# Two-stack hybrid network on one core: the second stack's opening norm in feature-major blocks, and a new order of the first microseconds

## The reference

```python
def hybrid_layer(x, ...):              # first stack
    h = rms_norm(x, norm_gain)
    proj = h @ w_in                    # attention in two kinds, gates ...
    y = sigmoid(gate_a) * (ua @ w_branch_a) + sigmoid(gate_b) * (ub @ w_branch_b)
    return x + y @ w_out

def second_block(x, meta_tokens, ln_in_g, ln_in_b, ...):
    h = concatenate([meta, x], axis=1)          # 16 + 256 tokens
    h = _layer_norm(h, ln_in_g, ln_in_b)        # mean and variance over the 2048 features
    for l in range(DEPTH):
        h = _hybrid_layer(h, pos, ...)          # convolution, windowed attention, recurrence
    return h[:, N_META:]                        # ends each layer in a _layer_norm too
```

## Time and profile before

| | us |
|---|---|
| median of the runs shown (3) | 3278.61 |
| lowest, highest | 3278.15, 3279.22 |
| the profiled execution, its own time | 3277.46 |
| its span, first to last instruction | 3275.7 |
| PE busy in that span | 3215.3 |
| DVE, ACT, POOL busy | 1989.7, 1652.3, 497.6 |

### The profile page before, as it was taken

How to read it: one execution, slowest core, us unless ns; L and a number is a source line. 1 busy time by engine, 2 the same in 40 slices (tenths; PEclk the granted TensorE clock), 3 DMA queues, 4 the chain that set the end, 5 groups by cost and what they waited for, 6 DMA issues and landing times.

```text
span 3275.7 us, 48063 instructions
## 1 busy us (share of the span) xinstructions
PE 3215.3 (98%) x17364; PEld 2782.6 (85%) x17364; DVE 1989.7 (61%) x2226; ACT 1652.3 (50%) x2291; POOL 497.6 (15%) x426
## 2 busy tenths in 40 slices
PE   8999999999999999999999999999987999999998
PEld 7888888888888888888888888888877999989997
DVE  5666655455544555766755555544546887668966
ACT  5445456555344445444555555444434566455654
POOL 4544500000000003554500000000002000010000
PEclk9999999999999999999999999999998999999998
DMA  6555555545655555555555555555553444544443
GB/s 230 173 173 183 174 169 173 179 160 179 193 193 192 186 200 181 173 173 173 184 174 171 170 175 173 193 193 193 186 169 139 153 139 139 174 170 150 153 155 116
DMA packets 157148, 566.90 MB, mean 173 GB/s; under 512 B 17536, under 2 KB 19728, under 8 KB 156752
## 3 DMA queue, kind: packets, MB, share of 16 engines
q1 hardware_dynamic: 155680, 558.00, 51.2%
q0 software_dynamic: 1344, 7.16, 0.6%
HBM read 562.99 MB, written 2.10 MB: 173 GB/s over the span
## 4 chain that ended last, share of the span: by engine, by line
PE 96%; DVE 2%; ACT 1%; POOL 1%; issue 0%; DMA 0%; SPq 0%; ACTq 0%; POOLq 0%; DVEq 0%
PE acc L1602 23%; PE acc L1604 23%; PE acc L1603 23%; PE acc L1856 6%; PE acc L1858 6%; PE acc L1857 6%; PE work L1662 1%; PE work L1835 1%; PE work L1919 1%; DVE w_lo L1023 1%; PE work L1836 1%; PE work L1837 1%; PE work L1947 0%; PE work L1719 0%; PE work L1670 0%; PE work L1673 0%
## 5 line engine op out<-in xcount | busy, mean ns | idle before, releaser
L1023 DVE TENSOR_TENSOR w_lo<-raw,w_hi 128x1024 fp32r<-128x1024 f32 x1056 | 1399.6, 1336 | 1025.7 <-ACT w_hi L606 870.9
L606 ACT ACTIVATE w_hi<-raw 128x1024 fp32r<-128x1024 f32 x832 | 874.4, 1057 | 903.3 <-PE acc L1604 903.3
L1602 PE MATMUL acc<-w_hi,hT_hi 128*128 128x512 f32 x2560 | 1014.7, 396 | 2.4 <-DVE hT_lo L1029 2.4
L1604 PE MATMUL acc<-w_hi,hT_lo 128*128 128x512 f32 x2560 | 999.0, 390 | 0.0
L1603 PE MATMUL acc<-w_lo,hT_hi 128*128 128x512 f32 x2560 | 997.5, 390 | 0.0
L1604 PEld LDWEIGHTS acc<-w_hi,hT_lo 128*128 128x128 f32 x2560 | 481.0, 188 | 102.9
L1602 PEld LDWEIGHTS acc<-w_hi,hT_hi 128*128 128x128 f32 x2560 | 481.6, 188 | 97.5 <-issue 2.8
L1603 PEld LDWEIGHTS acc<-w_lo,hT_hi 128*128 128x128 f32 x2560 | 481.8, 188 | 95.8
L620 ACT ACTIVATE w_hi<-raw 128x1024 fp32r<-128x1024 f32 x224 | 236.2, 1057 | 298.8 <-PE acc L1858 286.1
L1856 PE MATMUL acc<-h_hi,w_hi 128*128 128x272 f32 (+1 forms) x1152 | 336.5, 292 | 0.0
L1858 PE MATMUL acc<-h_hi,w_lo 128*128 128x272 f32 (+1 forms) x1152 | 329.9, 286 | 0.0
(11 more groups left out here) (314 smaller groups left out, 3636.8 us busy)
## 6 DMA issues: line engine op xcount, KB each, us to landing
raw<-weights SPq DMA_DIRECT2D x1056, 512.0 KB, 3.3
mat<-mats POOLq DMA_DIRECT2D x2, 1536.0 KB, 7.5
X<-x_in SPq DMA_DIRECT2D x8, 256.0 KB, 7.3
out<-out_rows SPq DMA_DIRECT2D x8, 256.0 KB, 2.5
par<-params POOLq DMA_DIRECT2D x2, 640.0 KB, 5.0
cst<-consts POOLq DMA_DIRECT2D x1, 704.0 KB, 4.8
cst<-consts POOLq DMA_DIRECT2D x1, 552.0 KB, 4.7
ropeC<-rope POOLq DMA_DIRECT2D x2, 256.0 KB, 5.1
```

Source lines behind the costliest of these rows:

```text
L606: act.activation(w_hi[:, slot, :], raw[:, slot, :], ACT.Copy).then_inc(hi_ready, 1)
L1023: dve.tensor_tensor(w_lo[:, s % RING, :], raw[:, s % RING, :], w_hi[:, s % RING, :], ALU.subtract)\
L1602: pe.matmul(o, stat[0][:, kc, token], hi, start=(kc == 0), stop=False)
L1604: ins = pe.matmul(o, stat[1][:, kc, token], hi, start=False, stop=(kc == KC - 1))
```

## The change

**Between the stacks.** The token-major norm is taken out. During the last output projection, as soon as a block of 512 features has been added to `X`, PE transposes it (`turn_in`, two feature blocks at a time) between the halves of the next blocks. ACT evacuates the first two turns, DVE the others. The mean over the first 512 features, times a factor (`shift`), is subtracted from everything, so that sums of squares stay small. Sums of the centred blocks and of their squares are gathered on DVE (`sum_in`, `in_sum`), the squares on ACT (`square_in`), and PE adds them up over the partitions with `ones_d` (`mean_part`). After the last block two more turns, two evacuations, two squares and one sum follow, and then the same routine as between the layers (`variance`, `normal_pairs` on DVE, `norm_root_of`, `high_pairs` on ACT), now written once for both. `h2` moves in memory to where `ubT` was, so that `F` and `PJ` come next to each other. POOL issues its three DMAs and sets its constants when the last `yT_lo` is made, which is ahead of most of the projection. The chunks of `first_half` no longer have transposes between them.

**At the start.** `kept` is loaded ahead of the first weights. DVE clears `U`; ACT makes an activation on one column of it, which brings its table load to the front; PE makes six products on it (`FIRST_WARM`). The first slot of weights is split in two halves of 512 columns, and PE's first six products wait only for the first of them (`first_lo`).

```diff
@@ SP
             sp.dma_start(cst[:, C_ID:C_ID + P], consts1[:, C_ID:C_ID + P]).then_inc(set_loaded, 16)
+            sp.dma_start(kept[:, :, :], kept1).then_inc(set_loaded, 16)
             for slot in range(RING):
                 sp.dma_start(raw[:, slot, :], weights[slot]).then_inc(raw_loaded[slot], 16)
-                if slot == 0:
-                    sp.dma_start(kept[:, :, :], kept1).then_inc(set_loaded, 16)
@@ POOL
-            pool.wait_ge(x_added, 4 * DEPTH)
+            pool.wait_ge(y_ready, 4 * DEPTH)
+            pool.wait_ge(yT_lo, 8 * DEPTH)
             pool.dma_start(cst2[:, :], consts2).then_inc(in2_loaded, 16)
@@ ACT, start
+                    act.wait_ge(const_set, 2)
+                    act.activation(small[:, 90:91], U[:, 0, 0:1], ACT.Copy)
                     act.wait_ge(set_loaded, 32)
-                    for f in range(8):
+                    act.wait_ge(raw_loaded[0], 16)
+                    act.activation(w_hi[:, 0, 0:512], raw[:, 0, 0:512], ACT.Copy).then_inc(first_hi, 1)
+                    h_hi(l, 0)
+                    act.activation(w_hi[:, 0, 512:HALF], raw[:, 0, 512:HALF], ACT.Copy).then_inc(hi_ready, 1)
+                    for f in range(1, 8):
                         split(u, f, f + 1)
                         h_hi(l, f)
@@ ACT, last projection and opening norm
+            def evac_in(f):
+                act.wait_ge(turned2, f + 1)
+                act.activation(F[:, 2 * f:2 * f + 2, META:TOK], work[:, f, :].rearrange("p (c n) -> p c n", c=2), ACT.Copy)\
+                    .then_inc(in_raw, 1)
+            def square_in(p, centered):
+                act.wait_ge(in_centered, centered)
+                act.activation(sqf[:, 2 * p:2 * p + 2, :], F[:, 2 * p:2 * p + 2, :], ACT.Square).then_inc(in_sq, 1)
...
+            act.activation(small2[:, 1:2], small2[:, 2:3], ACT.Sqrt)
+            square_in(6, 8)
+            square_in(7, 9)
+            act.wait_ge(in2_loaded, 48)
+            norm_root_of(0)
+            split2(3)
+            high_pairs(0, 0)
@@ DVE, end of the last projection
+            split(g0 + 18, 15, 16)
+            sum_in(6, sqf[:, 0:2, :], sqf[:, 0:2, :], sqf[:, 4:6, :])
+            dve.wait_ge(in_centered, 7)
...
+            sum_in(12, LNT[:, 3, :], sqf[:, 0, :], sqf[:, 1, :])
+            for n in range(3):
+                split(U2, n, n + 1)
+            dve.wait_ge(acc_ready, U2)
+            for a in range(2):
+                x = X[:, :, 1536 + 256 * a:1792 + 256 * a]
+                dve.tensor_tensor(x, acc[:, 2:4, 256 * a:256 * a + 256], x, ALU.add).then_inc(x_added, 1)
+            evac_in(6)
+            evac_in(7)
+            dve.wait_ge(in_sq, 8)
+            sum_in(13, sqf[:, 12:14, :], sqf[:, 12:14, :], sqf[:, 14:16, :])
...
+            normal_pairs(0, 0)
@@ PE, start
+                    pe.wait_ge(const_set, 2)
+                    for _ in range(FIRST_WARM):
+                        pe.matmul(work[:, 3, 0:256], U[:, 0, 0:P], U[:, 1, :], start=True, stop=True)
@@ PE, last projection
+            def turn_in(f, added):
+                pe.wait_ge(x_added, added)
+                for c in (2 * f, 2 * f + 1):
+                    for t in range(NT):
+                        o = c % 2 * SEQ + t * P
+                        ins = pe.transpose(work[:, f % 4, o:o + P], X[:, t, c * P:c * P + P], ident)
+                ins.then_inc(turned2, 1)
+            def mean_part(bank, src, start, stop):
+                return pe.matmul(work[:, bank, 0:TOK], ones_d[:, :], src, start=start, stop=stop)
...
+            out_halves(3, 0, 2)
+            turn_in(4, done + 3)
+            out_halves(3, 2, 3)
+            turn_in(5, done + 3)
+            out_halves(3, 3, 7)
+            pe.wait_ge(in_sum, 12)
+            mean_part(0, LNT[:, 0, :], True, False)
+            mean_part(1, LNT[:, 3, :], True, False)
+            out_halves(3, 7, 8)
+            turn_in(6, done + 4)
+            turn_in(7, done + 5)
...
-                    if l == 0 and kc + 4 < KC:
-                        turn_x(kc + 4)
```

More of the change, by code:

```diff
@@ L107 @@
 PREP = 32
+FIRST_WARM = 6
 def releases():
@@ L797, in _ @@
                 split(g0 + 16, 6, 13)
[L798 to L801, removed]
+                if l + 1 < DEPTH:
+                    for n in range(3):
+                        for f in (2 * n, 2 * n + 1):
+                            split(g0 + 16 + n, 13 + f % 2, 14 + f % 2)
                             h_hi(l + 1, f)
-                    split(g0 + 16 + n, 15, 21 if n < 2 else 16)
@@ L806, in square_in @@
[L806 to L813, removed]
-                split2(n)
[L815 to L819, removed]
+                        split(g0 + 16 + n, 15, 21 if n < 2 else 16)
@@ new lines, in _, with norm_root_of, scale_pair @@
+            square_in(0, 4)
+            split(g0 + 17, 18, 19)
+            square_in(1, 5)
+            split(g0 + 17, 19, 21)
+            split(g0 + 18, 13, 16)
+            square_in(4, 6)
+            square_in(5, 7)
+            def norm_root_of(q):
+                act.wait_ge(post_var, 2 * (q + 1))
+                k = FROM[q - 1] if q else 0
+                act.activation(rs2[:, k:TOK], rs2[:, k:TOK], ACT.Sqrt).then_inc(norm_root, 1)
+            def scale_pair(q, p):
+                act.wait_ge(post_mul, 8 * q + p + 1)
+                k = FROM[q - 1] if q else 0
+                for c in (2 * p, 2 * p + 1):
+                    f = F[:, c, k:TOK]
+                    gain, offset = (par2[:, a + c:a + c + 1] for a in (R2_POSTG, R2_POSTB)) if q else (gin[:, a + c:a + c + 1] for a in (0, KC))
+                    act.activation(f, f, ACT.Identity, scale=gain, bias=offset).then_inc(f_ready, 1)
@@ L1223, in _ @@
                             h_lo(l + 1, f)
-                    split(g0 + 16 + n, 15, 20 if n < 2 else 16)
-                if l + 1 < DEPTH:
+                        split(g0 + 16 + n, 15, 20 if n < 2 else 16)
                     split(g0 + 20, 0, 3)
-                add_x(l, 3)
-            dve.wait_ge(x_added, 4 * DEPTH)
-            dve.wait_ge(set2, 5)
-            groups = [(X[:, n, :], P) for n in range(NT)] + [(meta_rows[:, :], META)]
-            for n, (src, r) in enumerate(groups):
-                if n == 2:
-                    dve.wait_ge(in2_loaded, 48)
-                dve.tensor_reduce(mean_in[0:r, n:n + 1], src, AX.X, ALU.add).then_inc(in_sum, 1)
@@ L1237, in _ @@
[L1237 to L1245 removed]
+                    add_x(l, 3)
@@ L1263, in keys, with normal_pairs @@
+            def normal_pairs(q, n):
+                variance(q, 0)
+                for p in range(1, KC // 2):
+                    if p > 1:
+                        subtract(q, p, 0)
+                    multiply(q, p, 0)
+                    low(q, p - 1)
+                    if 2 <= p < 7:
+                        split2(n + 1 + p)
+                low(q, KC // 2 - 1)
+            normal_pairs(0, 0)
             def keys(l):
@@ new lines, in mean_part @@
+            def mean_part(bank, src, start, stop):
+                return pe.matmul(work[:, bank, 0:TOK], ones_d[:, :], src, start=start, stop=stop)
+            done = 4 * (DEPTH - 1)
+            pe.wait_ge(yb_ready, 4 * DEPTH)
+            out_halves(1, 0, 2)
+            turn_in(0, done + 1)
+            out_halves(1, 2, 3)
+            turn_in(1, done + 1)
+            pe.wait_ge(in2_loaded, 48)
+            for c in range(KC):
+                ins = pe.transpose(work[:, 2, c * META:c * META + META], meta_rows[:, c * P:c * P + P], ident[0:META, 0:META])
```

325 lines of the change are left out of this document (199 added, 126 removed).

## The result

| | before | after |
|---|---|---|
| median, us | 3278.38 (4 runs, 3277.11 to 3279.22) | 3257.35 (4 runs, 3256.16 to 3259.89) |
| ratio, 95% interval | | 0.9937 [0.9926, 0.9949] |
| profiled execution: time, span | 3277.46, 3275.7 | 3257.23, 3255.4 |

What follows compares the result with a forecast made beforehand. PE was taken to bound the kernel (96% of the last chain). −17.2 − 6.6 + 1.0 + 7.2 − 1.7 − 2.7 = −20.0 us gave 3257.4 for the profiled execution, median 3258.6 us, range 3253.5 to 3265.

Steps and rivals of the forecast that it cites:

- start, first product and clock: Kernel start: first product at 9.4 instead of 11.1, −1.7 us; warming products lift the clock, −2.7 us.
- what the projection takes on: Last projection: PE takes on six turns (3.2), sixteen `meta_rows` transposes (2.6) and three `ones_d` products (1.4), together +7.2 us.
- hole: Between the stacks: last product seen by DVE to next stack's first product shrinks from 29.6 to 12.4 us, −17.2 us.
- chunks with the clock: First 16 chunks of the second stack: 12 groups of transposes shed, −6.6 us; extra low clock, +1.0 us.
- the squares' path: Between the stacks: ACT, DVE, PE, DVE handling of squares arrives last ahead of `rs2`, formed at 5.3 us.
- Half of the low-clock time: Behind the hole: extra low clock of 0 to 2.8 us, half of it lost; +1.0 us taken.
- the term of the sixteen transposes of `meta_rows`: In the projection: 0.16 us each, from a range of 0.135 to 0.28; 2.6 us in all, at most 4.5.
- The tight place: Ahead of the last projection half: DVE's sums stand at 9.8 us, PE asks at 10.9, 1.1 us to spare.
- Rival 2: Projection waits because sums or splits are late by more than 1.1 us: 3260 to 3264 us, chance 0.12.
- two forecast terms: Kernel start: earlier first product, −1.7 us, and clock already lifted at that product, −2.7 us.
- Rival 1: Start: clock low at the first product, 2.7 us lost wholly or to a third: 3260.5 to 3261.3 us, chance 0.28.
- The other reason given for the rival: Start: by the Trainium skill transposes do not count as busy, so only the six products lift the clock.

Runs made afterwards that it cites:

- Experiment 2: Changed kernel with the start of the kernel before, so the new norm alone: 3259.07 us, ratio 0.9944 to the kernel before.
- the control: The changed kernel run again, unchanged, beside the three kernels with fillers: 3256.11 us, ratio 0.9935 to the kernel before.
- experiment 3: Changed kernel without the six warming products on zeros at the start: 3257.77 us, ratio 0.9941 to the kernel before.
- experiment 7: Changed kernel with 54 transposes of the identity, results unread, in the hole between the stacks: 3253.73 us, ratio 0.9928 to the kernel before.

## Why the prediction was right, and where its terms were off

The right-hand column is measured in the profiled execution of the changed kernel against that of before. The start is measured at the first block that is added in the projection (2385.02 before, 2381.49 after).

| step | forecast, us | measured, us |
|---|---|---|
| start, first product and clock | −4.4 | −4.3 at the first head, −3.5 at the projection |
| what the projection takes on | +7.2 | +5.6 (62.99 to 68.59) |
| hole | −17.2 | −17.0 (29.6 to 12.63) |
| chunks with the clock | −6.6 + 1.0 | −5.5 (32.25 to 26.76) |
| sum | −20.0 | −20.4 (2509.87 to 2489.47) |

**The hole** was right in its mechanism and its parts: `rs2` at 5.5 us (forecast 5.3), 7.11 from there (7.10), 12.6 in all (12.4), and the squares' path last. Experiment 2 has the same 12.62 us without the start.

**The chunks.** The transposes cost 6.3 us, not 6.6. The clock was low for 5.78 us behind the hole, where it had been low for 4.08 before, which takes back 0.8. Half of the low-clock time was said to be lost. The products are 0.227 us apart at the low level and 0.125 at the full one, so 0.45 of it is lost, and over the runs the chunks lie within 0.1 us of that line: 24.20 us with none, 25.80 with 3.73, 26.26 with 4.83, 26.82 with 6.01. The two errors, 0.3 in the transposes and 0.2 in the clock, cancelled by luck. Where the clock fell, it stayed low for 3.0 to 6.0 us at these two places over all the runs, and nothing here predicts how long; this sets how well such a sum can be made, about 1 us.

**The projection** was mis-sized, 1.6 us too dear. Nearly all of it is the term of the sixteen transposes of `meta_rows`, for which 2.6 us were taken and which lie in one row. Timeline of PE after the change:

```profile
2388.17 1.16 PE L1960 MATMUL work<-cst,meta_rows 16*128 16x16 f32 x16
2389.27 0.50 PE L1719 MATMUL acc<-w_hi,uaT_hi 128*128 128x512 f32 x1
```

They take 1.10 us from start to start, 0.07 each: much less than a transpose of `X`, with 128 columns (0.12 to 0.135), and the bound was wrongly put at 0.135 from below. A turn cost 0.48 (2431.66 to 2434.86, less 2.72), not 0.54. The tight place held: the last sum ends at 2445.41, PE asks at 2446.22, so 0.8 us of slack where 1.1 was forecast. Rival 2 did not happen.

**The start** met its two forecast terms (−1.5 and −2.8 for −1.7 and −2.7). By the projection 0.8 of it was lost again; the waits for QN, 1.7 us in two places where the control has 1.0 in one, account for 0.7. In the control the first block is added 4.7 us earlier than before (2380.32), and with the start alone 4.8 us (2380.19): there the start's gain arrives whole. So the 0.8 is a loss of that execution and not of the change. One working figure was wrong with no effect on the sum: `kept` does not need 4.47 us, and what held the first turn was the warming products. The path through the weights, the half split and the two halves of `hT` is the one that binds, as forecast; in the changed kernel's execution the late turn added 0.5 us to it (experiment 3).

**Rival 1** is open in one respect. Its condition, a low clock at the first product, came up in one profiled execution of five. In that one the weights landed last (ACT's split at 7.47, in the others at 6.72 to 6.89), and PE's pauses between the warming products and the first product are 2.00 us in sum (0.91 and 1.09), where the others have 1.45 (the changed kernel), 1.48, 1.33 and 1.63. With the table load late they are 3.10 us, and the clock fell there too. So the fall goes with the longer pauses, as the rival has it, but two executions do not show that they decide it. What the prediction set against the rival was misread: the pause that it calls 7.1 us was 7.64 us long, and the clock had fallen inside it, as the 0.69 from 2876 to 2880 shows, so that "3 us is much shorter" said less than it seemed. The other reason given for the rival, that transposes don't count, fell with experiment 7 as far as holding the clock goes.

The errors of the terms nearly cancel: the projection came out 1.6 us cheaper; the start 0.9, the hole 0.2 and the chunks 0.1 us dearer. For the profiled execution 3257.4 was forecast and 3257.23 measured. The median was forecast 1.15 us above it, as in the runs before, and lies 0.12 above: that makes the rest of the 1.25 us by which the forecast was too slow. The mechanism was right at each place; that the total agrees to 1.25 us is in part luck.

## What to carry to other kernels

Where the sums of a norm can be gathered during the projection ahead of it, what is left on PE's path is the way of its last block. Walk that path step by step with the durations of a like norm elsewhere in the trace; here it came out within 0.3 us. Behind a pause like the two here, add the clock: the low-clock time times one less the ratio of the two spacings (0.45 here). And where PE stands still as long as here, about 7 us, try products or transposes whose result nobody reads. They delayed nothing here, since they end ahead of what PE waits for, and products gave 2.2 us in one place and 2.1 more with the second.

## What the runs showed of the hardware

- A small transfer issued ahead of the 512 KB ones was there for PE 2.6 us after its issue (experiment 3), and 4.47 us after it from behind the first of them.
- The granted clock did not fall at once when PE stopped: in the changed kernel it averaged 0.78 from 2456 to 2460, PE idle since 2455.5, and 0.50 from 2460 to 2468.
- Transposes of four-byte numbers held the full clock (6.06 us of them, granted 1.00 throughout, experiment 7).
- Sixteen transposes of 16 × 16 took 1.1 us back to back.
- A table load without work behind it took 1.28 us, and the activation on the new table started at once (0.74 and 1.28 to 2.03).
